# An RWKV mixer reordered: k mixes and k tiles first, the lora products behind and among the r tiles, the kk norm ahead of the decay sums

## What is computed

```python
def rwkv7_mixer(h, mu, w_rkv, w0, w1, w2, a0, a1, a2, g1, g2, k_k, k_a, r_k, ...):
    h_prev = shift(h)                       # one token back
    dh = h_prev - h
    xs = h[None] + dh[None] * mu[:, None, None, :]      # six mixes: r k v w a g
    r, k, v = xs[0] @ w_r, xs[1] @ w_k, xs[2] @ w_v
    w_log = -softplus(-(w0 + tanh(xw @ w1) @ w2)) - 0.5
    decay = exp(-exp(w_log))
    a = sigmoid(a0 + (xa @ a1) @ a2)
    g = sigmoid(xg @ g1) @ g2
    kk = heads(k * k_k);  kk = kk / max(sqrt(sum(kk * kk)), 1e-12)   # per head of 64
    k = k * (1 + (a - 1) * k_a)
    ... scan over tokens with decay, kk, a, k, v, r ...
    bonus = sum(r * k * r_k) * v            # per head
```

## Time and profile before

| | us |
|---|---|
| median of 3 runs | 1676.58 |
| lowest, highest | 1671.02, 1678.82 |
| profiled execution: span of its instructions | 1676.4 |
| profiled execution: own device time | not given apart from the span |
| PE busy (matmul) | 1497.3 (89%) |
| PE weight load busy | 1389.3 (83%) |
| DVE busy | 1031.8 (62%) |
| ACT busy | 750.2 (45%) |
| POOL busy | 619.4 (37%) |
| mean granted TensorE clock | 0.945 of 2.4 GHz |
| RWKV mixer ahead of the solve (end of the norm mean to the first transposes) | 390.25 to 523.46 |

### The profile page before, as it was taken

The page is one execution under the profiler, slowest core; times in us unless marked ns, Lnnn a source line. Parts: engine busy times, 40 slices in busy tenths (PEclk is TensorE's granted clock), DMA queues, the critical chain, the costliest instruction groups (busy, mean ns, idle before and its releaser), DMA issues.

```text
span 1676.4 us, 32397 instructions
## 1 busy us (share of the span) xinstructions
PE 1497.3 (89%) x13606; PEld 1389.3 (83%) x13606; DVE 1031.8 (62%) x1565; ACT 750.2 (45%) x1185; POOL 619.4 (37%) x300
## 2 busy tenths in 40 slices
PE   5989899997998885899997568989999898989998
PEld 5888899985887773899986457979999787989998
DVE  4595477736284458477788766356762389357752
ACT  3466465532412332465541111455553357555643
POOL 5222366740010010386741000336764232237663
PEclk9999899998899997999998668999999999999999
DMA  5433355562342001375552001435556343335553
GB/s 150 151 126 102 101 177 187 183 183 75 106 145 77 4 10 44 102 209 187 177 163 70 1 1 39 135 105 184 192 169 198 110 142 101 127 123 180 176 190 112
DMA packets 212801, 210.07 MB, mean 125 GB/s; under 512 B 12272, under 2 KB 211904, under 8 KB 212672
## 3 DMA queue, kind: packets, MB, share of 16 engines
q1 hardware_dynamic: 210784, 206.65, 38.2%
q0 software_dynamic: 832, 1.13, 0.4%
q10 hardware_dynamic: 1056, 0.43, 0.1%
HBM read 207.15 MB, written 1.05 MB: 124 GB/s over the span
## 4 chain that ended last, share of the span: by engine, by line
PE 74%; DVE 17%; ACT 4%; issue 3%; ACTq 1%; POOL 1%; DMA 0%; DVEq 0%; POOLq 0%
PE psum L370 15%; PE psum L371 15%; PE psum L372 15%; PE psum L644 6%; PE psum L454 5%; DVE work L2145 4%; PE psum L646 3%; DVE w_low L353 3%; ACT w_high L345 2%; PE psum L2076 1%; PE psum L390 1%; PE psum L1345 1%; DVE work L1103 1%; PE psum L1456 1%; PE psum L1442 1%
## 5 line engine op out<-in xcount | busy, mean ns | idle before, releaser
L353 POOL TENSOR_TENSOR w_low<-ring,w_high 128x1024 fp32r<-128x1024 f32 (+1 forms) x184 | 511.4, 2780 | 921.0 <-ACT w_high L345 886.0
L370 PE MATMUL psum<-x_high,w_high 128*128 128x256 f32 x2048 | 593.2, 290 | 45.7 <-issue 31.0
L371 PE MATMUL psum<-x_low,w_high 128*128 128x256 f32 x2048 | 588.0, 287 | 0.0
L372 PE MATMUL psum<-x_high,w_low 128*128 128x256 f32 x2048 | 587.7, 287 | 0.0
L345 ACT ACTIVATE w_high<-ring 128x1024 fp32r<-128x1024 f32 (+1 forms) x368 | 361.8, 1034 | 262.1 <-PE psum L372 165.9
L370 PEld LDWEIGHTS psum<-x_high,w_high 128*128 128x128 f32 x2048 | 401.7, 196 | 53.1 <-issue 36.3
L371 PEld LDWEIGHTS psum<-x_low,w_high 128*128 128x128 f32 x2048 | 402.0, 196 | 1.0 <-issue 1.0
L372 PEld LDWEIGHTS psum<-x_high,w_low 128*128 128x128 f32 x2048 | 401.9, 196 | 0.0
L353 DVE TENSOR_TENSOR w_low<-ring,w_high 128x1024 fp32r<-128x1024 f32 (+1 forms) x184 | 251.8, 1370 | 176.9 <-ACT w_high L345 176.5
L730 DVE SCALAR_TENSOR_TENSOR work<-psum,par,work 128x255 f32<-128x255 f32 (+1 forms) x352 | 145.4, 475 | 155.1 <-ACT work L669 154.9
L644 PE MATMUL psum<-inner,w_high 128*128 128x512 f32 x528 | 186.5, 398 | 2.7 <-DVE w_low L353 2.7
(11 more groups left out here) (299 smaller groups left out, 1860.6 us busy)
## 6 DMA issues: line engine op xcount, KB each, us to landing
ring<-in_ffn_w_up_dram SPq DMA_DIRECT2D x88, 1024.0 KB, 5.1
ring<-in_ffn_w_down_dram SPq DMA_DIRECT2D x32, 1024.0 KB, 5.2
ring<-in_dsa_w_in_dram SPq DMA_DIRECT2D x28, 1024.0 KB, 5.2
ring<-in_ffn_w_down_dram SPq DMA_DIRECT2D x16, 768.0 KB, 4.6
ring<-in_rwkv_w_rkv_dram SPq DMA_DIRECT2D x12, 1024.0 KB, 5.1
ring<-in_dsa_w_out_dram SPq DMA_DIRECT2D x8, 1024.0 KB, 5.1
ring<-in_s_w_glu_dram SPq DMA_DIRECT2D x8, 1024.0 KB, 5.4
ring<-in_rwkv_w_out_dram SPq DMA_DIRECT2D x4, 1024.0 KB, 5.2
```

Of the source, the lines that this page charges most:

```text
L353: eng.tensor_tensor(low, raw, high.bitcast(F32), ALU.subtract).then_inc(sem("w_split", b), 1)
L370: pe.matmul(out_, lhs[0], rhs[0], start=start, stop=False, skip_group_check=True)
L371: pe.matmul(out_, lhs[0], rhs[1], start=False, stop=False, skip_group_check=True)
L372: return pe.matmul(out_, lhs[1], rhs[0], start=False, stop=stop, skip_group_check=True)
```

## The change

Five edits to the mixer of layer 1, and one to semaphores everywhere:

1. On DVE the difference and the mix of k are made chunk by chunk inside the norm's loop (`norm_scale` takes a callback); each chunk's mix waits for its own difference. The other mixes follow in the order w a g r v. The first norm of that layer is called from `rwkv_dve`.
2. On PE the order is k0 to k3, lora1, r0 (with the first two kk sums after its first half), lora2 for w, the other two kk sums, r1 (with lora2 for a after its first half), lora2 for g, r2, r3, v0 to v2, v3 (with two r·k sums after its first half), and the other two r·k sums. k0 waits for each chunk of the mix; lora1, r0 and v0 wait for the last chunk of theirs.
3. On DVE kk and its normalisation stand ahead of the decay sums.
4. On ACT the copies of k and squares of kk come first, then the hidden values, two roots, the copy of r0, two roots, the sigmoids of w and a, the copy of r1, the copies of g, the copy of r2, the exponentials, and the copies of r3 and v.
5. The weight tiles are sent in the new order of use, and banks are given by a list.
6. Some semaphores are merged or dropped (constants, the S5 parameters, the transposes of x), with waits on higher counts of the shared ones.

```diff
+RWKV_TILES = ([("k", i) for i in range(4)] + [("lora1", 0), ("r", 0), ("lora2", 0)] + [("r", i) for i in (1, 2, 3)] +
+              [("v", i) for i in range(4)])
+RWKV_FILLS = [("k", 0, 0), ("k", 1, 1), ("k", 2, 2), ("k", 3, 3), ("lora1", 0, 4), ("r", 0, 5),
+              ("w", 0, 0), ("w", 1, 1), ("w", 2, 2), ("w", 3, 3), ("r", 1, 4),
+              ("a", 0, 5), ("a", 1, 0), ("a", 2, 1), ("a", 3, 2), ("g", 0, 3), ("g", 1, 5), ("g", 2, 0), ("g", 3, 1),
+              ("r", 2, 2), ("r", 3, 4), ("v", 0, 3), ("v", 1, 5), ("v", 2, 0), ("v", 3, 1)]
...
+            for s, i in RWKV_TILES:
+                plan.weights((L, s, i), 3 if s in ("lora1", "lora2") else 1)
+            for s, i, bank in RWKV_FILLS:
+                plan.fill((L, s, i), bank)
...
-        def norm_scale(dve, n, gain, L):
+        def norm_scale(dve, n, gain, L, then=lambda c: None):
...
                     dve.scalar_tensor_tensor(out=hT[:, c, :], in0=xT[:, c, :], scalar=col(gain, L * DC + c),
                                              in1=rstd[:, :], op0=ALU.mult, op1=ALU.mult).then_inc(sem("h_ready"), 1)
+                then(c)
...
+            def kk_sums(first):
+                for m in (first, first + 1):
+                    pe.wait_ge(sem("kk_squares"), m + 1)
+                    if m >= 2:
+                        pe.wait_ge(sem("kk_root"), m - 1)
+                    pe.matmul(banks[6 + m % 2][:, :], sum_head[:, :], kk_sq[:, 2 * m:2 * m + 2, :], start=True,
+                              stop=True).then_inc(sem("kk_sum"), 1)
...
+            project(pe, (L, "k", 0), mixed["k"], lambda c: mix_ready("k", c))
+            for i in (1, 2, 3):
+                project(pe, (L, "k", i), mixed["k"])
+            lora_first()
+            mix_ready("r", DC - 1)
+            project(pe, (L, "r", 0), mixed["r"], halfway=lambda: kk_sums(0))
+            lora_second("w")
+            kk_sums(2)
+            project(pe, (L, "r", 1), mixed["r"], halfway=lambda: lora_second("a"))
+            lora_second("g")
+            project(pe, (L, "r", 2), mixed["r"])
+            project(pe, (L, "r", 3), mixed["r"])
+            mix_ready("v", DC - 1)
+            for i in range(3):
+                project(pe, (L, "v", i), mixed["v"])
+            project(pe, (L, "v", 3), mixed["v"], halfway=lambda: rk_sums(0))
+            rk_sums(2)
...
+            kk_roots(0)
             copy_out("r", 0)
+            kk_roots(2)
+            sigmoids("w", sg, "rwkv_w0")
+            sigmoids("a", aT, "rwkv_a0")
+            copy_out("r", 1)
+            for i in range(4):
+                key = (L, "g", i)
+                wait_full(act, key)
...
+            copy_out("r", 2)
+            act.wait_ge(sem("csum_done"), 2)
+            for dst, src, scale in ((e_prev, e_prev, 1.0), (e_in, csum, 1.0), (e_neg, csum, -1.0)):
+                act.activation(dst[:, :, :], src[:, :, :], ACT.Exp, scale=scale).then_inc(sem("exps_done"), 1)
+            copy_out("r", 3)
...
+            def difference(c):
+                wait_h(dve, n, c)
+                step.mark(dve.tensor_tensor(dh[:, c, 1:T], hT[:, c, 0:T - 1], hT[:, c, 1:T], ALU.subtract))
+                step.mark(dve.tensor_scalar(dh[:, c, 0:1], hT[:, c, 0:1], -1.0, None, ALU.mult))
+                return step.n
...
+            def first_mix(c):
+                if c:
+                    made = difference(c - 1)
+                    dve.wait_ge(step.sem, made)
+                    mix("k", c - 1)
+
+            norm_scale(dve, n, "norm_mix", L, first_mix)
+            for s in MIXES[1:]:
+                for c in range(DC):
+                    mix(s, c)
...
-                ins.then_inc(sem("z_ready"), 1)
-                dve.wait_ge(step.sem, step.n)
-                dve.wait_ge(sem("z_ready"), q + 1)
+                    else:
+                        dve.wait_ge(step.sem, step.mark(ins))
```

More of the change, by code:

```diff
@@ L143, in make_plan @@
         elif kind == 1:
[L144 to L151, removed]
+            for s, i in RWKV_TILES:
+                plan.weights((L, s, i), 3 if s in ("lora1", "lora2") else 1)
+            for s, i, bank in RWKV_FILLS:
+                plan.fill((L, s, i), bank)
+            for s, i in RWKV_TILES:
+                plan.used[(L, s, i)] = ("bank_full", plan.bank[(L, "g", 3) if s == "lora2" else (L, s, i)])
             simple([(L, "o", i) for i in range(4)], split=True)
@@ L1283, in second @@
                         (wide[:, D:2 * D], A["rwkv_g2"][0])]
-            send(sp, (L, "lora2", 0), second)
-            for s in "krv":
-                for i in range(4):
+            for s, i in RWKV_TILES:
+                if s == "lora1":
+                    send(sp, (L, s, i), first)
+                elif s == "lora2":
+                    send(sp, (L, s, i), second)
+                else:
                     send_plain(sp, (L, s, i), A["rwkv_w_rkv"][0, "rkv".index(s)], i * TILE)
@@ L1323, in rwkv_pe, with mix_ready, lora_first, lora_second @@
         def rwkv_pe(pe, L):
[L1325 to L1339, removed]
+            def mix_ready(s, c):
+                pe.wait_ge(sem("mixed"), MIXES.index(s) * DC + c + 1)
+            def lora_first():
+                key = (L, "lora1", 0)
+                w = landed(pe, key)
+                wait_free(pe, key)
+                bank = bank_of(key)
+                for dst, c0, c1, s in ((bank[0:HALF, 0:T], 0, HALF, "w"), (bank[HALF:P, 0:T], HALF, P, "a"),
+                                       (bank[:, T:2 * T], P, 2 * P, "g")):
+                    mix_ready(s, DC - 1)
+                    for k in range(DC):
+                        mm = pe.matmul(dst, w[:, k, c0:c1], mixed[s][:, k, :], start=k == 0, stop=k == DC - 1)
+                mm.then_inc(sem("bank_full", plan.bank[key][0]), 1)
+            def lora_second(s):
+                w = landed(pe, (L, "lora2", 0)).rearrange("p k n -> p (k n)")
+                pe.wait_ge(sem("lora_ready"), 3)
+                r, c0, x = {"w": (slice(0, HALF), 0, hidden[:, 0:T]), "a": (slice(HALF, P), 0, hidden[:, 0:T]),
+                            "g": (slice(0, P), D, hidden[:, T:2 * T])}[s]
                 for i in range(4):
@@ new lines, in rk_sums @@
+            def rk_sums(first):
+                for m in (first, first + 1):
+                    pe.wait_ge(sem("rk_done"), 2 * m + 2)
+                    if m >= 2:
+                        pe.wait_ge(sem("bonus_done"), m - 1)
+                    else:
+                        pe.wait_ge(sem("kk_root"), 4)
+                    pe.matmul(banks[6 + m % 2][:, :], sum_head[:, :], rk[:, 2 * m:2 * m + 2, :], start=True,
+                              stop=True).then_inc(sem("rk_sum"), 1)
+            project(pe, (L, "k", 0), mixed["k"], lambda c: mix_ready("k", c))
```

177 lines of the change are left out of this document (74 added, 103 removed).

## The result

| | before | after |
|---|---|---|
| median | 1677.78 us (8 runs) | 1666.43 us (8 runs) |
| lowest, highest | 1671.02, 1681.42 | 1664.89, 1670.32 |
| ratio to before, 95% interval | | 0.9936 (0.9922 to 0.9950) |
| profiled span | 1676.4 | 1663.5 |
| profiled execution's own time | not given | 1665.22 |

The kernel is 0.64% faster, 10.7 us by the ratio, where 13.4 was forecast. The forecast lies just above the interval, which allows 8.4 to 13.1 us. The two profiled spans differ by 12.9. The stage gave 14.2 there and the rest of the kernel took 1.3 back.

A forecast was written before the change was run, and what follows sets the result against it. TensorE, busy nearly without a break from 398.96 to 522.49 us, was taken as the bound. 4.4 (start) + 12.2 (excess) - 3.2 (k0) = 13.4 us; 1676.4 - 13.4 + 0.2 = 1663.2 us, range 1658 to 1671.

The forecast's parts named there:

- The start: Norm to first k product: TensorE starts at 394.6 us instead of 398.96, 4.4 us earlier (3.9 to 4.7).
- k0: First k tile on TensorE: goes at the pace of VectorE's mixes, 1.38 us a chunk, ending at 404.7 us.
- From there on: TensorE from 404.7 us to the last r·k sum: 104.3 us of work without a wait, ending at 509.0.
- The stage: RWKV mixer, end of the norm mean to the first transposes: 13.4 to 13.5 us shorter.
- its 12.2 us of excess: TensorE's old stretch, 123.5 against 111.3 us: 2.5 + 6.3 low clock and mix pace, 2.6 gap, 0.8 wait.
- everything behind the stage keeps its length: Kernel after the reordered part of the mixer: same length, only shifted in the clock's rhythm, allowed 4 us either way.
- The absolute time: Whole kernel: profiled span 1676.4 less 13.4, plus 0.2 from span to median, gives 1663.2 us; within 4 us, chance 0.67.
- the clock in the separated lora blocks: Rival: TensorE's clock falls in the separated 64-row lora blocks, costing 6.3 us, giving 1669.5; chance 0.09.
- the failed covers: Rival: r3's weights land late or VectorE's chain delays the sums, costing 3 to 6 us, 1666 to 1669; chance 0.12.
- the sticking clock: Rival: TensorE stays at 1.2 GHz through the k tiles and beyond, ending 10.8 us after today's, 1687; chance 0.04.
- The fourth: Rival: the following solve waits for late v copies or GpSimd's tails, costing up to 13 us, 1672 to 1677; chance 0.06.
- The lost overlap of w and a: lora2 on TensorE: separating w and a loses their row-group overlap; keeping them adjacent would save 0.86 us.

The follow-up runs named there:

- the last two runs: Changed kernel with k0 and k1 made together, chunk by chunk: ratio to before 0.9919; the same plus eight extra unread products before the first mix: 0.9909.
- the second profile of the kernel before: Kernel before, run again with no edit: ratio 0.9988, median 1677.06 us, norm mean to first transposes 130.1 us.
- the second comparison: Changed kernel timed again with no edit, against the kernel before on the same chip: ratio 0.9934, median 1669.28 us.
- two experiments: Kernel before with only k0 moved between lora1 and lora2: ratio 0.9941; kernel before with five extra unread products behind lora1: ratio 0.9959.

## Why the prediction was right, and where it was not

- *The start.* Forecast 4.35 us from the mean to the first k product, measured 4.30. The difference of one chunk was priced 0.40 and the column 0.17; in the chain they take 0.33 and 0.07. The norm products made up for it: the first starts 2.39 us behind the mean instead of 2.32, and the two take 0.88 instead of 0.81.
- *k0.* A chunk was forecast at 1.38 us and takes 1.31, all of the difference in the term of 0.40 that is 0.33; from the start of the column to the start of the mix behind it 0.18 pass, as priced. k0 ends 14.2 us behind the mean, forecast 14.45. The low spell lasted 3.4 us and cost nothing, as said; that it costs once TensorE has two tiles per chunk was shown by the last two runs.
- *From there on.* Forecast 104.3 us of work without a wait, measured 103.9 (405.2 to 509.06). The loras ran at 2.4 GHz. lora1 took 9.90 where 10.4 was summed, and lora2, in three blocks, 10.75 where 10.4 was, so that two small errors nearly cancel. The prediction also put part of lora1's excess down to the pace of the mixes. They were not in it: lora1 takes 9.90 us plus half of its time at the low clock, 12.92 with 6.1 us of it in the first profile and 11.43 with 3.0 in the second. None of the covers failed: the kk sums, the bank of a1, r3's weights and the r·k sums show no idle time of TensorE. VectorE's last factor came 71.8 us behind k3, forecast 71.7.
- *The stage.* Forecast 13.4, measured 14.2 in the pair of profiles. What I did not see is that the kernel before is not always so slow there: over its profiles and that of the semaphores alone the stage is 132.4 on average, which makes the gain 13.3. The working took its 12.2 us of excess from one profile of the long form; from the shorter one it would have come out some 3 us lower. That the profile at hand was of the commoner form, which four of the five of that order without a fill or a moved tile have, is luck.
- *The step that failed* is "everything behind the stage keeps its length". The reorder made the exponentials the last table of the stage, and the group norm pays a load. In all seven profiles of the changed order VectorE waits 2.69 to 2.70 us there; in all seven of the old order 1.27. I read ScalarE's table loads for the stage and did not ask which table it leaves behind. This is 1.4 us of the forecast, by the wait. That a root ahead of the v copies would win it back was not tried. The Trainium skill (ScalarE: Activation LUTs, What ACT_TABLE_LOAD costs) gives 1283 ns for a load and about 2.66 us for a switch with the drain that it adds. The trace has 1.28 us for the load, the root starts as it ends, and the wait grew by 1.42, so the drain does not show here.
- *The absolute time.* Forecast 1663.2, measured 1666.43. Of the 3.2 us, 1.2 are the median of the kernel before, which over eight runs is 1677.78 and not 1676.58; the other 2.0 are the difference of the medians, 11.4 in place of 13.4. I had put 0.2 us between span and time by setting a span beside the median of other runs; in each of the eight executions of the kernel after it is 1.7 to 1.8 (1665.22 and 1663.5 in the profiled one).
- *The sum as measured*: 13.3 - 1.4 = 11.9 us for the mixer, against 10.7 by the ratio (8.4 to 13.1) and 10.2 by the medians of the second comparison. The rest of the mixer is 1.6 us longer on average over the seven profiles of the new order (172.5) than over the seven of the old one (170.9). That looks like the load, but only half of it lies where the load does. From the first transposes to the group norm's first reciprocal the new order takes 114.9 on average and the old one 114.1, with the profiles of one order 2.1 to 3.5 us apart among themselves; from there to the end of the next norm mean, behind the load, 57.6 and 56.8. In that last piece TensorE was at the low clock for 30.7 us in all seven profiles of the new order and for 17.1 to 30.7 in those of the old. So the load is seen in the wait and on the chain, and how much of it reaches the end is not told apart from where the low spells fall. Some 1 us is left open.

Of the rivals, the clock in the separated lora blocks, the failed covers and the sticking clock did not come. The fourth, a gain given back behind the stage, did in part, by another mechanism than the one I named. The lost overlap of w and a is real and small: with the blocks side by side, at 2.4 GHz, lora2 takes 10.0 us in two experiments, and the three separate blocks together 3.65 + 3.65 + 3.45 = 10.75.

## What to carry to other kernels

A short gap of the tensor engine can cost more in clock than in idle time: here 2.6 us cost 9.3, and one tile of independent work put into it brought most of what a reorder of four engines did. An earlier start is worth only the work that the engine can do with what it is fed, so put first the product that has the most work per input and needs the fewest inputs, and give the engine two tiles per input if it is still starved. Read a stage from several profiles before putting a few us down to an edit. When activations are reordered, look at which function table is left behind at the end of the stage, and who pays for the next load.

## What the runs showed of the hardware that was not expected

- Filling the gap with products whose result nobody reads kept the clock at 1.00 and made a 16.7 us block 10.0 us long. With the gap open, the block was at 1.2 GHz for 10.2 or 13.6 us though TensorE was busy all the time, 10.8 us of them products of 64 rows in the first profile; started at 2.4 GHz, 7.3 us of such products in two blocks did not lower it. In the second profile of the kernel before the clock was still at 1.00 for the first 2.6 us behind the gap and fell then.
- The same order gave low spells of 6.8 and 10.2 us around the start of lora1, and of 10.2 and 13.6 us in lora2, from one execution to another. That is 3.2 us of the stage; the first three runs of the kernel before lay 7.8 us apart, and how much of that is the same effect is not shown. In the changed kernel, whose low spell lies where VectorE sets the pace, the stage had the same length in both profiles (119.05 and 119.08).
- Of the eight r·k products on VectorE six take 0.47 us and two 3.84, in the changed kernel from 485.75 to 493.35; GpSimd's two large products run from 485.58 to 493.07. With the rounds behind the decay sums both move by 10 us and the same two take 3.84 again.
- An operation on one column has a record of 0.15 us. In a row of others its end comes 0.07 us behind the end of the one before it, and the mix that waits for it starts 0.18 us after it started.
